# A retrieval stage whose products move: diagonals made behind their own dots, some products on VectorE, and x1 added last

## The reference, cut to what matters

```
def peer_ffn(h, wq, k1, k2, u, v):
    q = (tb @ wq).reshape(P_BLOCK, P_HEADS, P_DKEY)
    s1 = einsum('thd,nd->thn', q[..., :half], k1)
    s2 = einsum('thd,nd->thn', q[..., half:], k2)
    v1, i1 = top_k(s1, 16)
    v2, i2 = top_k(s2, 16)
    ...
    sc, pos = top_k(cand, P_TOPK)
    g = softmax(sc)
    pre = einsum('td,thkd->thk', tb, u[idx])
    act = gelu(pre) * g
    return einsum('thk,thkd->td', act, v[idx])
```

## Time and profile before

| what | value |
|---|---|
| median of the runs | 4864.03 us |
| profiled execution, its own time | 4865.45 us |
| span of its trace | 4863.9 us |
| TensorE, VectorE, ScalarE, GpSimd busy | 4346.6, 3060.0, 988.9, 1446.3 us |
| first and last dot | 1848.2 and 4812.0 us |
| mean granted TensorE clock | 0.959 |

### The profile page before, as it was taken

The page is one execution under the profiler, slowest core; times in us unless marked ns, Lnnn a source line. Parts: engine busy times, 40 slices in busy tenths (PEclk is TensorE's granted clock), DMA queues, the critical chain, the costliest instruction groups (busy, mean ns, idle before and its releaser), DMA issues.

```text
span 4863.9 us, 50927 instructions
## 1 busy us (share of the span) xinstructions
PE 4346.6 (89%) x17061; PEld 2692.7 (55%) x17061; DVE 3060.0 (63%) x7074; ACT 988.9 (20%) x2578; POOL 1446.3 (30%) x1391
## 2 busy tenths in 40 slices
PE   7999999999788788999999999878987988989877
PEld 7998777888655675546444545423433434434332
DVE  3444214666376436767668677677777777777784
ACT  2222111234355201110111111111211111112112
POOL 1000002222111002433344344344443444444441
PEclk8999999999899999999999999999999999999999
DMA  2223222444222459999999999999999999999995
GB/s 91 84 75 121 94 83 83 135 126 129 74 80 80 139 178 342 380 388 395 412 393 406 379 410 412 413 413 407 383 405 420 377 406 420 400 414 405 393 411 223
DMA packets 399898, 1383.49 MB, mean 284 GB/s; under 512 B 38240, under 2 KB 214096, under 8 KB 264496
## 3 DMA queue, kind: packets, MB, share of 16 engines
q0 software_dynamic: 167728, 1166.48, 59.7%
q1 hardware_dynamic: 231936, 214.03, 13.6%
HBM read 1299.91 MB, written 80.49 MB: 284 GB/s over the span
## 4 chain that ended last, share of the span: by engine, by line
PE 34%; DMA 19%; DVE 8%; issue 4%; SPq 1%; POOL 1%; ACT 1%; DVEq 0%; POOLq 0%; ACTq 0%
PE peer_acc L2516 20%; DMA peer_uv<-in_peer_uv_dram,peer_idx 17%; PE peer_fo L2454 5%; PE peer_fo L2397 3%; PE peer_fo L2467 2%; PE peer_tb L2350 2%; DVE peer_uv L1939 1%; DMA peer_space<-in_w_attn_o_dram 1%; DVE peer_diag L1954 1%; DMA peer_space<-in_w_out_dram 1%; PE peer_fo L2407 1%; DVE peer_hot L1897 1%; DVE peer_hot L1900 1%; DVE peer_sel L1903 1%; PE peer_sb L2360 0%
## 5 line engine op out<-in xcount | busy, mean ns | idle before, releaser
L2516 PE MATMUL peer_acc<-peer_uv,peer_diag 128*128 128x512 f32 (+1 forms) x4224 | 2032.9, 619 | 269.1 <-DVE peer_diag L1954 267.7
L1806 POOL DMA_INDIRECT peer_uv<-in_peer_uv_dram,peer_idx x1056 | 1201.2, 1138 | 1798.7 <-PE peer_acc L2516 1695.3
L1939 DVE CUSTOM_DVE_ANT_0 peer_uv<-peer_uv,peer_h 128x1024 f32<-128x1024 f32 x1056 | 1291.7, 1223 | 703.3 <-DMA peer_uv<-in_peer_uv_dram,peer_idx 697.1
L2516 PEld LDWEIGHTS peer_acc<-peer_uv,peer_diag 128*128 128x128 f32 (+1 forms) x4224 | 782.9, 194 | 1293.8 <-issue 767.0
L2311 ACT ACTIVATE peer_ge<-peer_pre 128x1 f32<-128x1 f32 x1056 | 213.1, 203 | 2495.0 <-DVE peer_pre L1939 2488.6
L2454 PE MATMUL peer_fo<-peer_space 128*128 128x256 f32 (+2 forms) x1152 | 401.0, 476 | 50.6 <-DVE peer_space L2014 18.8
L1954 DVE TENSOR_SCALAR peer_diag<-ident,peer_ge,peer_gw 128x128 f32<-128x128 f32 x1024 | 352.5, 344 | 10.5 <-ACT peer_ge L2311 9.0
L99 PE MATMUL proj_bank<-proj_hTh,proj_wplead 128*128 128x352 f32 x1008 | 356.9, 354 | 0.1
L2454 PEld LDWEIGHTS peer_fo<-peer_space 128*128 128x128 f32 x1152 | 222.0, 197 | 216.8 <-issue 161.8
L100 PE MATMUL proj_bank<-proj_hTr,proj_wplead 128*128 128x352 f32 x1008 | 328.0, 325 | 0.0
L101 PE MATMUL proj_bank<-proj_hTh,proj_wprest 128*128 128x352 f32 x1008 | 327.9, 325 | 0.0
(11 more groups left out here) (326 smaller groups left out, 5258.1 us busy)
## 6 DMA issues: line engine op xcount, KB each, us to landing
proj_wp<-in_w_in_dram POOLq DMA_DIRECT2D x13, 2048.0 KB, 9.9
peer_space<-in_w_ssm_o_dram SPq DMA_DIRECT2D x48, 512.0 KB
peer_uv<-in_peer_uv_dram,peer_idx POOLq DMA_INDIRECT x1056
proj_wp<-in_w_in_dram POOLq DMA_DIRECT2D x14, 1024.0 KB, 8.2
peer_space<-in_w_attn_o_dram SPq DMA_DIRECT2D x24, 512.0 KB
peer_space<-in_w_out_dram SPq DMA_DIRECT2D x24, 512.0 KB
scratch_xtok<-proj_shared SPq DMA_DIRECT2D x20, 512.0 KB, 3.2
scratch_chan<-proj_stg SPq DMA_DIRECT2D x48, 176.0 KB
```

The source lines that it names most:

```text
L1806: pool.indirect_dma_start(uv[k][:], None, io["peer_uv"], bass.IndirectOffsetOnAxis(ap=idx[t % 2][:, col:col + 1], axis=0)).then_inc(uv_in[ ...
L1939: dve.tensor_tensor_reduce(uv[k][:, 0:D], uv[k][:, 0:D], h2[t % 2][:], 1.0, 0.0, ALU.mult, ALU.add, pre[g % 2][:, k:k + 1]).then_inc(u_don ...
L2516: x = pe.matmul(acc[0:r, h:h + HALF], diag[k][:, 0:r], uv[k][:, D + h:D + h + HALF], start=False, stop=last)
```

## The change

1. `slot(n)` on VectorE is now: dot of slot n, the mixing of slot n, diagonal of slot n itself. The diagonal waits for the Gelu of the same slot.
2. In tiles 0 and 1, from the third iteration on, every fourth slot is an aside: no diagonal and no product. VectorE multiplies `ge` by the weight (128x1) and adds that factor times the `v` half to x1 in SBUF. GpSimd's fetch into such a buffer waits for `aside_done`; `products(n)` counts the slots up to n that still have a product.
3. TensorE no longer opens with x1. The first product starts the accumulation, and x1 is added behind the last product of the tile, which counts `closed`. SyncE loads the next x1 at slot 2 of the tile, behind `closed`.
4. ScalarE copies the sum behind the first Gelu of the next tile, no longer the second.
5. The heads of queries go to slots 0 and 4 of iterations 2 to 5, the scores to iterations 5 and 7, and ScalarE's copies follow.

```diff
-    HEAD_AT = ((2, 0), (2, 2), (2, 4), (2, 6), (3, 0), (3, 2), (3, 4), (3, 6))
+    HEAD_AT = ((2, 0), (2, 4), (3, 0), (3, 4), (4, 0), (4, 4), (5, 0), (5, 4))
...
+    ASIDE_TILES, ASIDE_FROM, ASIDE_EVERY = 2, 2, 4
+    def aside(n):
+        t, at = n // PSLOT, n % PSLOT
+        return t < ASIDE_TILES and at >= ASIDE_FROM * SLOTS and n % ASIDE_EVERY == ASIDE_EVERY - 1
+    asides = [sum(map(aside, range(n + 1))) for n in range(SLOTS * TOTAL)]
+    def products(n):
+        return n + 1 - asides[n]
...
-                        if at == 12 + SLOTS * LATE[t + 1]:
-                            sp.wait_ge(opened, t + 1)
-                            load_x1(t + 1)
...
+                    if at == 2 and t:
+                        sp.wait_ge(closed, t)
+                        load_x1(t)
...
-                        pool.wait_ge(v_done, n - SLOTS + 1)
+                        if aside(n - SLOTS):
+                            pool.wait_ge(aside_done, asides[n - SLOTS])
+                        else:
+                            pool.wait_ge(v_done, products(n - SLOTS))
...
+                def add_aside(t, g, it, k):
+                    q = asides[g * SLOTS + k]
+                    if q > 1:
+                        dve.wait_ge(aside_done, q - 1)
+                    dve.tensor_tensor(factor[:], ge[g % 2][:, k:k + 1], gw[t % 2][:, it * SLOTS + k:it * SLOTS + k + 1], ALU.mult).then_inc(aside_step, 1)
+                    dve.wait_ge(aside_step, q)
+                    dve.wait_ge(x1_in, 16 * (t + 1))
+                    dve.scalar_tensor_tensor(out=x1[:], in0=uv[k][:, D:2 * D], scalar=factor[:, 0:1], in1=x1[:],
+                                             op0=ALU.mult, op1=ALU.add).then_inc(aside_done, 1)
...
                     dve.wait_ge(gelu_done, g * SLOTS + k + 1)
+                    n = g * SLOTS + k
+                    if aside(n):
+                        add_aside(t, g, it, k)
+                        return
                     if g:
-                        dve.wait_ge(v_done, (g - 1) * SLOTS + k + 1)
+                        dve.wait_ge(v_done, products(n - SLOTS))
...
                     dots(t, g, k)
-                    if n:
-                        weights(*places[n - 1])
+                    mixing(n)
+                    weights(t, g, it, k)
...
-                    act.wait_ge(v_done, FIRST[t + 1] * SLOTS)
+                    act.wait_ge(closed, t + 1)
...
-                            if t and it == 0 and k == 1:
+                            if t and it == 0 and k == 0:
                                 sum_out(t - 1)
...
-                    elif (it, k) == (4, 1):
+                    elif (it, k) == (5, 1):
                         scores(0, n * PREP_ACT + 3)
-                    elif (it, k) == (5, 1):
+                    elif (it, k) == (7, 1):
                         scores(1, n * PREP_ACT + 6)
...
-                    pe.wait_ge(x1_in, t * 16 + 16)
                     if t:
                         pe.wait_ge(acc_out, t)
-                    for h in range(0, D, HALF):
-                        x = pe.matmul(acc[0:r, h:h + HALF], c.ident[0:r, 0:r], x1[0:r, h:h + HALF], start=True, stop=False)
-                    x.then_inc(opened, 1)
...
+                            if not aside(n):
+                                pe.wait_ge(diag_done, products(n))
+                                pe.wait_ge(uv_in[k], g * 16 + 16)
+                                for h in range(0, D, HALF):
+                                    x = pe.matmul(acc[0:r, h:h + HALF], diag[k][:, 0:r], uv[k][:, D + h:D + h + HALF],
+                                                  start=(it == 0 and k == 0), stop=False)
+                                x.then_inc(v_done, 1)
+                    pe.wait_ge(x1_in, t * 16 + 16)
+                    if asides[n]:
+                        pe.wait_ge(aside_done, asides[n])
+                    for h in range(0, D, HALF):
+                        x = pe.matmul(acc[0:r, h:h + HALF], c.ident[0:r, 0:r], x1[0:r, h:h + HALF], start=False, stop=True)
+                    x.then_inc(closed, 1)
```

More of the change, by code:

```diff
@@ L1534, in segments_at @@
         return [(tile, n // SEGS, n % SEGS) for tile in range(NT) for n in range(PAIRS * SEGS) if due(tile, n) == g]
+    ASIDE_TILES, ASIDE_FROM, ASIDE_EVERY = 2, 2, 4
[5 more added lines that the diff above has]
+        return n + 1 - asides[n]
     def heads_scored(tile, pair):
         j1 = pair >= PAIRS // 2
-        if tile == 0:
-            return PREP_ACT if j1 else 5
-        return tile * PREP_ACT + (PREP_ACT if j1 else 6)
+        return tile * PREP_ACT + (PREP_ACT if j1 else 5)
     with Stage(nc, "peer") as s:
@@ L1608, in retrieve_and_finish @@
         u_done, v_done, gelu_done, diag_done = (s.sem(n) for n in ("u_done", "v_done", "gelu_done", "diag_done"))
-        opened, acc_out, x2_stored, x2f_in = s.sem("opened"), s.sem("acc_out"), s.sem("x2_stored"), s.sem("x2f_in")
+        closed, acc_out, x2_stored, x2f_in = s.sem("closed"), s.sem("acc_out"), s.sem("x2_stored"), s.sem("x2f_in")
         gain_in, ffn_in, gains = s.sem("gain_in"), s.sem("ffn_in"), s.sem("gains")
@@ L1905, in choose @@
                         if t >= 2:
-                            dve.wait_ge(v_done, FIRST[t - 1] * SLOTS)
+                            dve.wait_ge(v_done, products(FIRST[t - 1] * SLOTS - 1))
                         dve.scalar_tensor_tensor(out=idx[t % 2][:, 2 * p * PTOP:(2 * p + 2) * PTOP].rearrange("p (e a) -> p e a", e=2),
@@ L2144, in _ @@
                             slot(g * SLOTS + k)
-                            mixing(g * SLOTS + k)
                         for tile, p, part in todo[0:1]:
@@ L2164, in _ @@
                             finish(t - 1, "mean")
-                weights(*places[-1])
                 finish(LAST - 1, "out")
@@ L2261, in prepare_piece @@
                         rows_out(n)
-                    elif it == 3:
+                    elif it == 4:
                         queries_out(n, 0, n * PREP_PE + 3)
-                    elif it == 4:
-                        queries_out(n, 1, n * PREP_PE + 4)
-                        scores_out(n, 0, n * PREP_PE + 5)
                     elif it == 5:
+                        scores_out(n, 0, n * PREP_PE + 4)
+                    elif it == 6:
+                        queries_out(n, 1, n * PREP_PE + 5)
+                    elif it == 7:
                         scores_out(n, 1, n * PREP_PE + 6)
@@ L2510, in _ @@
                             finish_piece(t, it, k)
-                            mixing(g * SLOTS + k + PE_AHEAD)
-                            pe.wait_ge(diag_done, g * SLOTS + k + 1)
-                            pe.wait_ge(uv_in[k], g * 16 + 16)
-                            last = it == TILE_ITS[t] - 1 and k == SLOTS - 1
-                            for h in range(0, D, HALF):
-                                x = pe.matmul(acc[0:r, h:h + HALF], diag[k][:, 0:r], uv[k][:, D + h:D + h + HALF], start=False, stop=last)
-                            x.then_inc(v_done, 1)
+                            mixing(n + PE_AHEAD)
+                            if not aside(n):
[11 more added lines that the diff above has]
+                    x.then_inc(closed, 1)
                 finish(LAST, "embedding")
```

2 lines of the change are left out of this document (added).

## The result

The changed kernel takes 4887.38 us (median of 13 runs, 4874.28 to 4897.77), the kernel before 4872.49 us beside it (13 runs, 4862.35 to 4888.28). The ratio is 1.0025, 95% interval 1.0014 to 1.0036: **slower by a quarter of a per cent**, some 12 us. The forecast was 4862 us and a wash. The time lies in its range (4836 to 4892); the direction was missed.

A forecast was written before the change was run, and what follows sets the result against it. The gathers' transfers were taken as the bound, so gains come only from time without them. Losses 9+8+4+2 = 23 us against gains 22.5+1.5 = 24 gave net -1, rounded towards the gains to 4862 us, range 4836 to 4892.

The forecast's parts named there:

- a wash: Whole kernel: gains and losses nearly cancel, 4862 us, own range 4854 to 4873; chance 0.39.
- SP's wait for `closed` at slot 2 holds its later loads for at most those slots; x1 has 16 slots to land for tile 1's first aside: 0: SyncE's queue at a tile's start: waiting for the closed sum before loading the next x1 costs 0.
- A slot costs VectorE 1.75 us in place of 1.40: VectorE in busy rows: the diagonal waits for its own Gelu, +0.35 us a slot, 370 us over 1,056; free in quiet stretches.
- theories A and B: From the experiments, not the forecast: A, asides overfill VectorE; B, the wait of a slot's own diagonal costs.
- Tile 0, +9: Tile 0's window: VectorE's busiest stretches overfill with the diagonal's wait and asides, 9 us lost, from 0 to 20.
- Tile 1, +8: Tile 1: VectorE has 105.1 us of work in 94.9, less the cushion's 2.2; 8 us lost, from 0 to 18.
- Tile 7, +4: Tile 7, where the last tile's choosing is dense: VectorE overfills, table loads on top; 4 us lost, from 0 to 12.
- the larger cushion: Gather buffers: released about 2.2 us earlier, so products may fall that much further behind the 13.6 us before transfers stop.
- Gaps, 22.5 won: Stretches where transfers pause: spread queries and the cushion shrink them by 22 to 23 us, outside tile 0's balance.
- Boundaries +2, end 0, start +1.5: x1 closing the sum: 2 us lost at tile boundaries, 0 at the end (or +2), 1.5 gained at the start.
- ScalarE's table loads: Exponential blocks between dot and diagonal: two loads of 1.283 us, about 3.2 us a block; VectorE stands 2.2 when busy.
- Rival (c): VectorE becomes the bound through table loads and asides: 4899 us, milder half 4885; chance 0.30.

The follow-up runs named there:

- e13: Changed kernel with asides from slot 24 of a tile in place of 16, x1's load still at slot 2: 4882.49 us, ratio 1.0018 to the kernel before.
- e7: Changed kernel with x1's wait and load at slot 14 in place of 2, asides from slot 24 in place of 16: 4873.09 us, ratio 0.9997.
- e11: Changed kernel with asides from slot 24, SyncE's wait for `closed` at slot 2 but x1's load at slot 14: 4871.45 us, ratio 0.9997.
- e1: Changed kernel without asides, every slot of tiles 0 and 1 keeping its diagonal and product: 4876.62 us, ratio 0.9998 to the kernel before.
- e9: e7 without asides, so the changed kernel without asides and with x1's load at slot 14: 4866.63 us, ratio 0.9982.
- e5: Changed kernel without asides and with a slot's diagonal a dot late, as before; x1's load stays at slot 2: 4868.64 us, ratio 0.9983.
- e8: e7 with all diagonals a dot late, as in the kernel before: 4860.81 us, ratio 0.9973 (0.9959 to 0.9988).
- e6: e5 with the wait for `closed` and x1's load at slot 14 in place of 2: 4865.17 us, ratio 0.9977.
- e12: e7 with the diagonals of tiles 0 and 1 only a dot late, as before; from tile 2 on a slot's own: 4869.0 us, ratio 0.9982.
- again: Second profiled execution of the changed kernel, unaltered, from its repeat run beside the others: 4885.89 us, ratio 1.0020.
- e2: Changed kernel with only VectorE's order put back, the diagonal or aside of slot n-1 behind the dot of slot n: 4871.25 us, ratio 0.9994.
- e4: Kernel before with only the queries spread over four iterations, scores and ScalarE's copies moved along: 4867.41 us, ratio 0.9990.
- e10: e7 with each gather also waiting for the next slot's product, as if one buffer of eight were gone: 4947.7 us, ratio 1.0131.

## Why the prediction was wrong

**The step that failed is "SP's wait for `closed` at slot 2 holds its later loads for at most those slots; x1 has 16 slots to land for tile 1's first aside: 0".** It looked at whom the load is for, and at the time for which SyncE stands. It did not ask what is queued behind the load. There stand the weights of the mixing and the stores of its x1, and VectorE's norm waits for those. In place of 0 it cost 1.0018 - 0.9997 = 0.21% or 10 us (e13 against e7 and e11), and 0.16%, 8 us, without asides (e1 against e9). The intervals within each pair touch, but that of the change (1.0014 to 1.0036, four asides more) lies above those of e7 and e11 (up to 1.0009), and the windows of tile 1 are far apart. It shows in tile 1 only, which lost 395.9 - 386.0 = 9.9 and 391.0 - 378.1 = 12.9 us there. e11 shows that the standing was rightly put at 0 and the transfer wrongly. With this one step mended the kernel comes out at 0.9997, the wash that was forecast. That it lands there is in part luck: in e7 tiles 0 and 1 cost 9.8 us where 17 were forecast, and tiles 2 to 7 won 11.3 where 22.5 - 4 = 18.5 were. Two errors of some 7 us cancel.

It needs company: with diagonals late and no asides (e5) the load at slot 2 did no harm that shows. The difference is already there in the issues. In e5 the load of x1 stands at the same place, and the stores are out 38.9 us behind the first weights:

```profile
2263.79 0.37 SPq L1690 DMA_DIRECT2D peer_space<-in_w_ssm_o_dram  x1
2272.44 0.81 SPq L1656 DMA_DIRECT2D peer_x<-scratch_x  x1
...
2297.85 0.34 SPq L1708 DMA_DIRECT2D peer_space<-scratch_yg  x1
2298.24 4.48 SPq L1721 DMA_DIRECT2D scratch_x<-peer_space  x3
```

That VectorE must be near full for the harm is argued from e5, not shown by itself.

Why an issue takes 9.62 us where it took 0.34 is not settled. The rows show that one transfer more is ahead of it in the same queue while the gathers keep the engines full, and that the same instructions are short again without it. But long issues are not made by the load of x1 alone: the changed kernel has them in tile 0 too, ahead of that load (up to 27.2 us), and the kernel before has some of up to 19.6. What the queue's limit is no run here tells.

The other steps:

- *A slot costs VectorE 1.75 us in place of 1.40.* Right in a busy row: 1.76 in the rows above. The diagonals' idle time behind the gate was forecast at 350 to 450 us; they are 306.7, where they were 9.0. What they cost depends on the company. Own against late diagonal is 0.9997 against 0.9973 with asides (e7, e8), and 0.9982 against 0.9977 without (e9, e6), where the intervals overlap. By the medians it costs about 12 us beside asides and 2 without, and 7 of the 12 in tiles 0 and 1, where the asides are (e12). That points to theories A and B being one: each affordable alone, both together too much for VectorE. It is argued, not shown: the intervals of e7 and e8 still touch (0.9986, 0.9988), those of e7 and e9 as well (0.9991), that of e12 overlaps both, and one stall comes and goes in tile 0.
- *Tile 0, +9.* Measured +6.7 and +4.6 (again), within the spread of such windows. The size came about right, but in part by luck: both traces hold the stall at the end of the tile, which the sum does not have, and the two with asides and without it are below the kernel before (-7.9 in e2, -4.8 in e12, both with late diagonals there). PE was forecast near 83% and stands at 355.5 of 423.2 us, 84%.
- *Tile 1, +8.* Measured +16.9 and +14.4. With the load moved it is 386.0 - 379.7 = 6.3 (e7): the term for VectorE was right and the rest is the load.
- *Tile 7, +4.* Measured +5.5 and +7.0. Over the four kernels with the late diagonal and the closing (e2, e5, e6, e8) tile 7 takes 342.9 us on average (341.0 to 344.1), over the eight with the own one 346.9 (344.6 to 348.0): +4.0. Not in the sum was the last tile, where the same averages are 90.9 and 94.4: +3.5. Tiles 4 and 5 go the other way, by -4.0 and -3.9 (339.6 to 335.6, 342.9 to 339.0). I take that for the larger cushion (argued, not tried), and it returns what tile 7 and the last lose.
- *Gaps, 22.5 won.* The second term that was mis-sized. Tiles 2 to 7 won 10.0, or 14 if tile 7's +4 is taken out first, and the queries alone gave 9.5 of it (e4: 2079.7 against 2089.2). The windows that answer to the earlier trace rows show which gaps stayed:

```profile
1927.30:1977.30 50.00, 40.49 (x135) 24.42 (x136) 46.75 (x134) 4.81 (x19) 14.97 (x14) 0.86 0.81 308
...
3420.00:3470.00 50.00, 50.00 (x153) 25.12 (x152) 38.09 (x97) 8.07 (x23) 19.92 (x16) 1.00 0.92 347
...
3810.00:3860.00 50.00, 50.00 (x177) 26.77 (x176) 34.96 (x74) 10.73 (x30) 19.56 (x18) 1.00 0.92 360
4540.00:4600.00 60.00, 51.84 (x124) 22.80 (x125) 48.99 (x140) 10.88 (x33) 21.01 (x20) 0.94 0.89 348
```

  By the prediction's own formula they lost 10.3, 4.9, 4.9 and 7.6 us, where the earlier trace rows had 8.3, 6.2, 7.8 and 3.9. The forecast had 1, 3 and 2 for the last three. The sign "no share below 0.9" at tile 5's queries failed too: from 3819 to 3829 us it is 0.80. That tile is shorter by 5.4 us, and by 3.1 again, where 5 to 8 were named. In the gaps at 3420 and 3810 TensorE still has both bursts at once: of the worst ten microseconds (3819 to 3829) the gate products take 3.2 and the queries 1.9. So whether the gate products alone would make a gap is not shown. The one at 4550 grew; it is there in e6, with the late diagonal and no asides, too (share 0.52 in its worst ten microseconds). Why was not tried.
- *Boundaries +2, end 0, start +1.5.* VectorE was to stand 1 to 3 us more at each of the first boundaries, as Gelu 1 is now behind the copy. It stands 7.5, 5.7 and 3.8 us there (7.5, 5.4 and 5.1 again), before at most 1.8. What of it reaches the time no run tells: e6 has 6.9 and 6.0, and the ratio 0.9977. From the last dot to the end of the span it was 51.9 us before and 52.1 after. Here the 0 holds.
- *ScalarE's table loads.* The row of one is 1.283 us as before (L2277, nine loads, all 1283 ns). The trace of the kernel before has a switch to the root's table and back:

```profile
3705.21 0.20 ACT L2311 ACTIVATE peer_ge<-peer_pre 128x1 f32<-128x1 f32 x1 [1.22 <-DVE peer_pre L1939]
3705.43 1.28 ACT L2233 ACT_TABLE_LOAD   x1
3706.72 0.20 ACT L2233 ACTIVATE peer_ft<-peer_fss 128x1 f32<-128x1 f32 x1
3706.94 1.28 ACT L2311 ACT_TABLE_LOAD   x1
```

  From the first Gelu's end at 3705.41 to the end of the second load at 3708.22 are 2.81 us for two loads and one activation. That leaves no room for two switches at the 2.66 us of the Trainium skill (ScalarE: Activation LUTs, What ACT_TABLE_LOAD costs); here the measurement decides, and the sum was right to go by the row.
- *The chances.* Rival (c), VectorE as the bound at 4885 to 4899, gives the measured time, but not for its reasons. It put tile 1 at up to +18 through VectorE's work; the work gave 6, and a transfer 10. The named sign "if tiles 3 to 6 grow" did not come for the four together (-2.9, -6.0, -5.4, +2.6). Tile 6 grew a little, but by as much with the queries alone (+3.1, e4).

**What a better version is.** The gain is that of the spread queries (0.9990 alone), with perhaps a little from the closing with x1 loaded behind the stores (0.9977 for both, intervals overlapping). The asides add nothing that shows (e6 0.9977, e8 0.9973), and beside the own diagonal they seem to cost (e7). e8, or e6 as the simpler one, is 0.23 to 0.27% faster than before and some 0.5% faster than the change (0.9973 against 1.0020 to 1.0025). The interval of e8 ends at 0.9988, so the gain is real and small.

## What to carry to other kernels

A transfer that is moved in an issuing queue must be costed for everything behind it, not only for its own reader: list the next five or six issues of that engine and ask who waits for each, stores included. Two edits that each use up the slack of one engine (here +0.35 us a slot and +1.25 us every fourth slot) are best summed against that slack once, together; the runs point to this, without showing it. And where buffers release gathers, the depth in flight outranks the finer points of order: one slot's delay cost 1.3% (e10), more than all parts of this change moved. And before a row marked x2 is called a long issue, ask for its single instructions.

## What was not expected of the hardware

Beside the gathers (share about 1, some 400 GB/s) an issuing instruction of SyncE lasts from 0.30 to 27.18 us (the latter at 2060.06 in the changed kernel). The issue of the same rows load takes 20.39 us in the changed kernel and 0.34 in e9. From issue to landing a weights load or a store of x1 takes 16.9 us (median) in e7, two issued last in that list 31.7 and 34.1. So a chain of store, wait and load costs far more there than its bytes.

Removing one buffer's worth of lead from the gathers (e10) did not lower the contention for the others; it stretched tile 0 by 12.2 us and tile 1 by 18.9 against e7.
